# Regrouping the SSD side products of a hybrid SSD / S5 decoder step on one Trainium2 core

## The reference, cut to what matters

```python
cb = einsum('bcqgn,bcsgn->bcqsg', cm, bm)
y_diag = einsum('bcqsgj,bcsgjp->bcqgjp', cb[..., None] * seg, xdt)
states = einsum('bcsgn,bcsgjp->bcgjpn', bm, xdt * decay[..., None])
h = chunk_decay * h + states
y_off = einsum('bcqgn,bcgjpn->bcqgjp', cm, h_prev) * exp(acs)[..., None]
```

## Time and profile before

| | |
|---|---|
| median of 3 runs | 2355.67 us (2355.64 to 2357.68) |
| the profiled execution | 2355.64 us, of which the span from first to last instruction is 2353.9 us |
| PE busy | 2346.1 us, 100% of the span |
| DVE, ACT, POOL busy | 1651.4 us (70%), 1060.0 us (45%), 109.2 us (5%) |
| DMA | 453.95 MB, mean 193 GB/s |
| one iteration of the groups | 100.67 us, from one t = 0 stay to the next (575.66 to 676.33) |

### The profile page before, as it was taken

The page is one execution under the profiler, slowest core; times in us unless marked ns, Lnnn a source line. Parts: engine busy times, 40 slices in busy tenths (PEclk is TensorE's granted clock), DMA queues, the critical chain, the costliest instruction groups (busy, mean ns, idle before and its releaser), DMA issues.

```text
span 2353.9 us, 49580 instructions
## 1 busy us (share of the span) xinstructions
PE 2346.1 (100%) x19158; PEld 2299.7 (98%) x19158; DVE 1651.4 (70%) x3109; ACT 1060.0 (45%) x1583; POOL 109.2 (5%) x202
## 2 busy tenths in 40 slices
PE   9999999999999999999999999999999999999999
PEld 9999999999999999999999999999999999999998
DVE  7798988979888878798956555765555555544444
ACT  6453544535444445646633333554334333333333
POOL 1000000000000002101300000000000000000000
PEclk9999999999999999999999999999999999999999
DMA  7676767677676678566876765555555555555543
GB/s 215 199 225 206 242 189 216 212 214 235 189 225 212 206 239 241 152 194 177 250 204 193 205 211 182 182 171 161 162 169 160 170 162 159 174 197 168 169 159 117
DMA packets 546113, 453.95 MB, mean 193 GB/s; under 512 B 31184, under 2 KB 520112, under 8 KB 545408
## 3 DMA queue, kind: packets, MB, share of 16 engines
q1 hardware_dynamic: 525936, 406.23, 57.4%
q0 software_dynamic: 13392, 34.33, 4.5%
q10 hardware_dynamic: 6624, 11.18, 1.4%
HBM read 412.01 MB, written 38.81 MB: 192 GB/s over the span
## 4 chain that ended last, share of the span: by engine, by line
PE 97%; DVE 2%; issue 0%; ACT 0%; POOL 0%; DVEq 0%; ACTq 0%; POOLq 0%
PE acc L2097 30%; PE acc L2098 29%; PE acc L2099 29%; PE side L2084 1%; PE side L2183 1%; PE side L2235 1%; PE side L2107 0%; DVE cacc L1343 0%; PE side L2400 0%; PE side L2366 0%; PE side L2217 0%; PE acc L2579 0%; PE side L2579 0%; PE side L2577 0%; PE side L2578 0%
## 5 line engine op out<-in xcount | busy, mean ns | idle before, releaser
L1298 DVE TENSOR_TENSOR w_lo<-raw,w_hi 128x1024 fp32r<-128x1024 f32 (+2 forms) x692 | 830.2, 1207 | 513.2 <-ACT w_hi L793 507.7
L793 ACT ACTIVATE w_hi<-raw 128x1024 fp32r<-128x1024 f32 (+2 forms) x692 | 716.6, 1045 | 850.9 <-PE acc L2099 828.4
L2097 PE MATMUL acc<-h_hi,w_hi 128*128 128x288 f32 x3344 | 999.5, 299 | 0.0
L2099 PE MATMUL acc<-h_hi,w_lo 128*128 128x288 f32 x3344 | 986.0, 295 | 0.0
L2098 PE MATMUL acc<-h_lo,w_hi 128*128 128x288 f32 x3344 | 985.2, 295 | 0.0
L2097 PEld LDWEIGHTS acc<-h_hi,w_hi 128*128 128x128 f32 x3344 | 627.8, 188 | 15.5 <-issue 13.3
L2098 PEld LDWEIGHTS acc<-h_lo,w_hi 128*128 128x128 f32 x3344 | 627.4, 188 | 2.2 <-issue 2.2
L2099 PEld LDWEIGHTS acc<-h_hi,w_lo 128*128 128x128 f32 x3344 | 627.8, 188 | 0.0
L2097 PE MATMUL acc<-f_hi,w_hi 128*128 128x288 f32 x698 | 207.0, 296 | 0.0
L2099 PE MATMUL acc<-f_hi,w_lo 128*128 128x288 f32 x698 | 205.7, 295 | 0.0
L2098 PE MATMUL acc<-f_lo,w_hi 128*128 128x288 f32 x698 | 205.4, 294 | 0.0
(11 more groups left out here) (406 smaller groups left out, 2681.1 us busy)
## 6 DMA issues: line engine op xcount, KB each, us to landing
raw<-in_w_in_dram SPq DMA_DIRECT2D x512, 256.0 KB, 3.5
raw<-in_w_ffn_up_dram SPq DMA_DIRECT2D x352, 256.0 KB, 3.4
raw<-in_w_ffn_down_dram SPq DMA_DIRECT2D x160, 256.0 KB, 2.9
raw<-in_w_ssm_out_dram SPq DMA_DIRECT2D x128, 256.0 KB, 3.4
raw<-in_w_glu_dram SPq DMA_DIRECT2D x128, 256.0 KB, 3.7
h<-in_state_ssm_dram SPq DMA_DIRECT2D x32, 512.0 KB, 6.9
out_ssm_sample_dram<-h POOLq DMA_DIRECT2D x32, 512.0 KB, 3.8
raw<-in_w_out_dram SPq DMA_DIRECT2D x64, 256.0 KB, 3.2
```

The source lines that it names most:

```text
L793: copy = lambda out, in_, **k: nc.scalar.activation(out, in_, ACT.Copy, **k)
L1298: tt(w_lo[:, slot, 0:n], raw[:, slot, 0:n], w_hi[:, slot, 0:n].bitcast(F32), ALU.subtract).then_inc(lo_ready, 1)
L2097: mm(o_, wh, xh[:, kt, :], start=first and i == 0, stop=False)
L2099: done = mm(o_, wl, xh[:, kt, :], start=False, stop=last and i == n - 1)
```

## The change

SSD operations move to other steps, and some to other banks. Nothing is added or removed but a few waits.

| | before | after |
|---|---|---|
| PE: turns of the x sample rows | t = 6 | t = 3, alone |
| PE: `within` of blocks 0, 1, 2 | t = 6, 6, 12 | t = 8 (s2, s0, s1) |
| PE: reads of the sample states | t = 12 | t = 8 |
| PE: block 0's state | t = 6, into s1 | t = 10, into s2, alone |
| PE: block 1's reads, block 1's state | t = 8, into s1, s3 | t = 12, into s1, s0 |
| PE: turns of the sample reads | t = 14 | t = 12 |
| ACT: copy of block 0's state; of the sample reads | t = 7; 13 | t = 11; 9 |
| DVE: sample x; mask of block 2; `cm` | t = 7; 7; 10 | t = 5; 6; 7 |
| DVE: skips of blocks 0, 1, 2 | t = 9, 11, 13 | t = 9, 9, 10 |
| DVE: block 1's reads scaled, added; samples' | t = 11, 12; 15 | t = 13, 13; 13 |
| DVE: `ht` decayed and added (`prompt_state_ready`) | t = 10 | t = 14 |
| DVE: decays of the sample states | t = 13 to 16 | t = 11, 12, 14, 15 |
| SP: loads of the sample states | t = 6 to 9 | t = 4 to 7 |

PE's wait for `prompt_state_ready` moves from t = 12 to t = 16. SP's wait for it stays at t = 17.

```diff
@@ -464,8 +464,8 @@
                     conv_history(g + 1)
                 if not ssd:
                     return
-                if 6 <= t < 10:
-                    q = t - 6
+                if 4 <= t < 8:
+                    q = t - 4
                     if g > 0:
                         sp.wait_ge(h0_stored[q], g * 16)
                     sp.dma_start(h0[:, 2 * q:2 * q + 2, :], a['state_ssm'][g, :, 2 * q:2 * q + 2, :]).then_inc(h0_landed[q], 16)
@@ -871,13 +871,13 @@
                     if t == 8:
                         act.wait_ge(sem("xw_ready"), g * 3 + 3)
                         copy(xws[0:32, :], offe[0:32, :]).then_inc(sem("xws_rounded"), 1)
-                    if t == 7:
+                    if t == 11:
                         act.wait_ge(sem("ht_ready"), g + 1)
                         act.wait_ge(sem("bst_ready"), g + 1)
-                        copy(ht[:, :], s1[:, :]).then_inc(sem("ht_copied"), 1)
-                    if t == 13:
+                        copy(ht[:, :], s2[:, :]).then_inc(sem("ht_copied"), 1)
+                    if t == 9:
                         act.wait_ge(sem("h0_read"), g + 1)
-                        act.wait_ge(sem("off1_added"), g + 1)
+                        act.wait_ge(sem("xws_ready"), g + 1)
                         copy(offe[:, :], s3[:, :]).then_inc(sem("read_copied"), 1)
                     if t == 24:
                         act.wait_ge(sem("y_gated"), g + 1)
@@ -1435,7 +1435,7 @@
                     if t == 4:
                         dve.wait_ge(sem("btok_ready"), g + 1)
                         tt(bst[32:64, :], ht[0:32, 0:NS], bst[0:32, :].bitcast(F32), ALU.subtract).then_inc(sem("bst_ready"), 1)
-                    if t == 7:
+                    if t == 5:
                         dve.wait_ge(sem("x2_turned"), g + 1)
                         tt(by_head(xdt[0:32, 2, :]), by_head(s3[0:32, :]), bc(gtv[0:32, DT + 2, :], HD, 2),
                            ALU.mult).then_inc(sem("xdt_ready"), 1)
@@ -1449,43 +1449,43 @@
                         mask(0, g)
                     if t == 5:
                         mask(1, g)
-                    if t == 7:
+                    if t == 6:
                         mask(2, g)
                     if t == 9:
                         dve.wait_ge(sem("y0_ready"), g + 1)
                         wait(dve, "y_summed", g * 3)
                         skip(0, s2, g, par)
-                    if t == 11:
-                        dve.wait_ge(sem("xws_ready"), g + 1)
-                        dve.wait_ge(sem("off1_ready"), g + 1)
-                        dve.wait_ge(sem("decay_landed"), g * 32 + 32)
-                        tt(offe[:, :].rearrange("p (i q) -> p i q", i=4), s1[:, :].rearrange("p (i q) -> p i q", i=4),
-                           ee[:, :, 0:P], ALU.mult).then_inc(sem("off1_scaled"), 1)
                         dve.wait_ge(sem("y1_ready"), g + 1)
                         skip(1, s0, g, par)
-                    if t == 10:
+                    if t == 7:
                         wait(dve, "h0_read", g)
                         cT = xc[:, par, 1, SEQ:T].rearrange("p (r h t) -> p h r t", h=2, t=DL)
                         for h in range(2):
                             last = dve.tensor_copy(cm[:, 4 * h:4 * h + 4, DL * h:DL * h + DL], cT[:, h])
                         last.then_inc(sem("cm_ready"), 1)
+                    if t == 13:
                         dve.wait_ge(sem("off1_ready"), g + 1)
-                        link(tt(by_head(ht[:, :]), by_head(ht[:, :]), bc(gtv[:, CDEC, :], HD, 2), ALU.mult))
-                        dve.wait_ge(sem("prompt_state"), g + 1)
-                        tt(ht[:, :], ht[:, :], s3[:, :], ALU.add).then_inc(sem("prompt_state_ready"), 1)
-                    if t == 12:
+                        dve.wait_ge(sem("off2_ready"), g + 1)
+                        dve.wait_ge(sem("decay_landed"), g * 32 + 32)
+                        tt(offe[:, :].rearrange("p (i q) -> p i q", i=4), s1[:, :].rearrange("p (i q) -> p i q", i=4),
+                           ee[:, :, 0:P], ALU.mult).then_inc(sem("off1_scaled"), 1)
+                        dve.wait_ge(sem("off1_scaled"), g + 1)
                         dve.wait_ge(sem("y_skip"), g * 3 + 2)
                         v = yb[:, :, P:SEQ]
                         tt(v, v, offe[:, :].rearrange("p (i q) -> p i q", i=4), ALU.add).then_inc(sem("off1_added"), 1)
                     if t == 14:
+                        link(tt(by_head(ht[:, :]), by_head(ht[:, :]), bc(gtv[:, CDEC, :], HD, 2), ALU.mult))
+                        dve.wait_ge(sem("prompt_state"), g + 1)
+                        tt(ht[:, :], ht[:, :], s0[:, :], ALU.add).then_inc(sem("prompt_state_ready"), 1)
                         dve.wait_ge(sem("outer_landed"), 16 * (g + 1))
                         tt(bm[:, :, :], bc(xwe[:, 512:].bitcast(F32), 2, 1), bc(hmask[:, 0:2], NS, 2), ALU.mult).then_inc(sem("bm_ready"), 1)
-                    if t == 13:
+                    if t == 10:
                         dve.wait_ge(sem("y2_ready"), g + 1)
-                        skip(2, s2, g, par)
-                    if 13 <= t < 17:
+                        skip(2, s1, g, par)
+                    if t in (11, 12, 14, 15):
                         dve.wait_ge(sem("h0_read"), g + 1)
-                        for u in (2 * (t - 13), 2 * (t - 13) + 1):
+                        first = 2 * (11, 12, 14, 15).index(t)
+                        for u in (first, first + 1):
                             of = bdec[:, SAMPLES[u], g * HG:(g + 1) * HG]
                             tt(by_head(h0[:, u, :]), by_head(h0[:, u, :]), bc(of, HD, 2), ALU.mult).then_inc(sem("h0_decayed"), 1)
                     if t in (17, 18, 21, 22):
@@ -1494,8 +1494,8 @@
                             dve.wait_ge(sem("h0_decayed"), g * DB + u + 1)
                             dve.wait_ge(sem("h0_product"), g * DB + u + 1)
                             tt(h0[:, u, :], h0[:, u, :], product_bank(u)[:, :], ALU.add).then_inc(sem("h0_updated"), 1)
-                    if t == 15:
-                        dve.wait_ge(sem("off2_ready"), g + 1)
+                    if t == 13:
+                        dve.wait_ge(sem("off1_added"), g + 1)
                         tt(offe[:, 0:P].rearrange("p (i r k) -> p i r k", i=4, r=4),
                            s3[:, :].rearrange("p (i r x) -> p i r x", i=4, r=4)[:, :, :, 0:2 * DL],
                            ee[:, :, P:160].rearrange("p i (r k) -> p i r k", r=4), ALU.mult).then_inc(sem("off2_scaled"), 1)
@@ -2204,37 +2204,36 @@
                             for i in range(4):
                                 last = turn((s2, s3)[c][:, i * P:(i + 1) * P], xc[:, par, 2 + i, c * P:(c + 1) * P])
                         last.then_inc(sem("x01_turned"), 1)
-                    if t == 6:
-                        pe.wait_ge(sem("btok_ready"), g + 1)
+                    if t == 3:
                         pe.wait_ge(sem("xdt_ready"), g * 3 + 2)
                         for i in range(4):
                             last = turn(s3[0:32, i * P:(i + 1) * P], xc[:, par, 2 + i, SEQ:T])
                         last.then_inc(sem("x2_turned"), 1)
+                    if t == 8:
+                        pe.wait_ge(sem("btok_ready"), g + 1)
+                        pe.wait_ge(sem("cb_masked"), g + 1)
+                        pe.wait_ge(sem("xdt_ready"), g * 3 + 3)
                         within(s2, 0, g).then_inc(sem("y0_ready"), 1)
                         within(s0, 1, g).then_inc(sem("y1_ready"), 1)
-                        pe.wait_ge(sem("cb_masked"), g + 1)
-                        pe.wait_ge(sem("xw_ready"), g * 3 + 2)
-                        mm(s1[:, :], btok[:, 0, :], xw[:, 0, :], **one).then_inc(sem("ht_ready"), 1)
-                    if t == 8:
-                        pe.wait_ge(sem("ht_copied"), g + 1)
-                        for i in range(4):
-                            last = mm(s1[:, i * P:(i + 1) * P], ht[:, i * P:(i + 1) * P], cT[:, P:SEQ], **one)
-                        last.then_inc(sem("off1_ready"), 1)
-                        pe.wait_ge(sem("xdt_ready"), g * 3 + 3)
-                        mm(s3[:, :], btok[:, 1, :], xw[:, 1, :], **one).then_inc(sem("prompt_state"), 1)
-                    if t == 12:
-                        pe.wait_ge(sem("xdt_ready"), g * 3 + 3)
-                        pe.wait_ge(sem("y_skip"), g * 3 + 1)
-                        within(s2, 2, g).then_inc(sem("y2_ready"), 1)
+                        within(s1, 2, g).then_inc(sem("y2_ready"), 1)
                         pe.wait_ge(sem("cm_ready"), g + 1)
-                        pe.wait_ge(sem("prompt_state_ready"), g + 1)
                         for b in range(DB):
                             if b % 2 == 0:
                                 pe.wait_ge(h0_landed[b // 2], g * 16 + 16)
                             r = b % 4
```

(13 more changed lines are left out.)

## The result

| | before | after |
|---|---|---|
| median | 2357.54 us (2355.64 to 2358.08, 5 runs) | 2395.55 us (2391.70 to 2397.65, 5 runs) |
| ratio, 95% interval | | 1.0166 (1.0155 to 1.0177), slower |
| span of the profiled execution | 2353.9 us | 2390.0 us |
| PE's granted clock, mean, profiled execution | 1.000 | 0.995 |
| one iteration | 100.67 us | 105.5 to 106.0 us |

Slower, as forecast, but by 36.1 us of span where 17.4 were forecast, and outside the range of 2360 to 2390. By the medians it is 38.0 us: the profiled execution is the fastest of the five, and the granted clock of the others was 0.993 or 0.994. The kernel before has two groups of runs, near 2355.7 and near 2357.8 us, and its median of five falls into the upper one.

What follows compares the result with a forecast made beforehand. PE, busy for the whole span, was taken as the bound. Group 0's 2.9, plus 14.6 for iterations 1 to 6, minus 0.1 for group 7, gave +17.4 us on 2355.64: 2373.0, range 2360 to 2390.

Steps and rivals of the forecast that it cites:

- The cause: SP's wait at t = 17 holds chunk 18's load, delaying DVE and PE's restart: +2.4 us in each of iterations 1 to 6.
- PE's stays: PE's time on the moved SSD work per group: 8.14 us before, 8.04 to 8.24 after; gain taken 0.1.
- the turns alone: PE's turns of the x sample rows, alone at t = 3 after the change, priced at 0.53 us.
- the rule on draining: On PE, each change of tiling mode drains the engine; ten changes per group before and after, so no gain.
- the chain: DVE's steps up to `z_silu`: 0.55 us leaves t = 15, 0.3 of the t = 16 decays is gained, together 0.9.
- the landing: Chunk 18's load, issued by SP after the store, lands 3.3 us later (median of 2.5 to 7.1), at 635.3.
- The lag at `z_silu`: DVE's `z_silu` before PE's hand-over starts 3.6 - 0.9 = 2.7 us late, at 675.1.
- The estimate of 2.6 us: Skill's DMA cost model for a 256 KB load: each hand-over 0.7 us sooner, 2368 in all; not adopted.
- my rival of the burst: Released SP queue makes chunks 19 and 20 land late, up to 3.8 us more per hand-over: 2386 to 2400; chance 0.13.
- the clock's rival: After each PE wait the next chunk runs at 1.2 GHz, 3.2 us more seven times, +22: 2395; chance 0.05.
- Group 0: Hand-over where PE already waits: split 4.6 us late, 0.55 and 1.2 come off, +2.9 all on the path.

Runs made afterwards that it cites:

- The late store: Changed kernel with SP's wait for the prompt's state and its store moved from t = 17 to t = 24: 2358.18 us, ratio 1.0009.
- the gate alone: Kernel before, with SP at t = 17 also waiting for the fourth decay of the sample states, nothing else moved: 2396.46 us, ratio 1.0166.
- late acs loads: Changed kernel with SP's four acs loads at t = 22 to 25 instead of 18 to 21: 2383.52 us, ratio 1.0117.
- store at t = 18: Changed kernel with SP's wait and store of the prompt's state at t = 18 instead of t = 17: 2367.24 us, ratio 1.0043.
- only the store behind chunk 18: Changed kernel with SP's wait left at t = 17 and only the store moved behind chunk 18's load, to t = 18: 2397.38 us, ratio 1.0169.
- store in POOL's queue: Changed kernel with the prompt's state wait and store moved from SP's queue to POOL's, ahead of its sample-state stores: 2358.26 us, ratio 1.0009.

## Why the prediction fell short

- **The cause was right**, step by step. The prompt's addition ends 55.4 us from the t = 0 stay, as computed (631.1 - 575.66). SP's wait at t = 17 holds the load of chunk 18, ACT's rounding ends on a DMA, and PE waits for the second z at seven places. The late store and the gate alone show it from both sides.
- **PE's stays** cost 0.44, 4.45, 0.86 and 2.19 us, 7.94 together, against 8.14: a gain of 0.2 per group where 0.1 was taken. The difference is the turns alone, 0.44 where I had priced 0.53. By the rule on draining (TensorEngine Tiling (Array Packing), the Trainium skill, Key Properties) the gain would be nil, as the prediction worked out; the measurement decides.
- **DVE without the gate** starts the split of t = 15 1.5 us later than before (58.7 against 57.2) and `z_silu` 0.65 later, so that 0.9 come off the chain, as computed.
- **The first step that failed is the landing.** I took 3.3 us, the median of loads that come two at a time, for a load that is let go together with a store, four acs loads and three more chunks. The second load of chunk 18 took 4.0 and that of chunk 19 6.4. The split of t = 15 came 4.3 us late in the iteration shown, not 3.6, and chunk 19 was late as well: of the 0.9 us by which the chain is lighter only 0.3 was left. The lag at `z_silu` was 4.04 us (100.74 from the stay, 96.70 before) instead of 2.7, PE's restart 3.77 late instead of 2.4. The estimate of 2.6 us that the prediction sets beside the 3.3 lies further off still. This was my rival of the burst, with a chance of 0.13, at 1.3 us per hand-over where I had given it 1.9 to 3.8. My argument against it, that DVE wants the chunks 3 to 5 us apart, missed that the chunk that comes first is short of time already.
- **The second is the clock**, which the sum put at nothing. It fell after six of seven waits of 3.35 us, at 1.34 us each in the iteration shown. I had this as a rival at 0.05, on the ground that a wait of 0.89 us did nothing, and put it beside the forecast instead of on it. The page TensorE: Matmul & The Clock Gate (the Trainium skill, Why this matters for your kernels) warns of just this, and the trace agrees. The two rivals were not exclusive: the longer wait brings the fall. That the sum of the clock's rival, 2395, is the measured time is luck: it rests on 3.2 us per fall, more than twice what one cost.
- **The sum, by the trace.** PE's restarts after the seven waits come 27.5 us late in all, where 17.5 were forecast (2.9 + 14.6; six times 2.4 is 14.4, so 0.2 of that was a slip). The six falls add 8.2, the first matmul after a restart about 0.1 in six iterations. The last t = 0 stay is then 36.2 late (813.23 against 777.00), the span 36.1. By kind of wait it comes out less well: 23.4 + 1.9 + 1.4 - 0.9 = 25.8, falls 8.2, stays -1.6, together 32.4 of 36.1. The rest fits the 13 waits that are new, near 0.27 us each beyond the idle time shown: a matmul's record lasts 0.29 where the next one starts after 0.13, and the first distance after a wait is 0.24. That reading was not tested by itself.
- **Group 0** was forecast at +2.9 and gave 5.4 (178.39 - 172.96): PE's restart came 4.1 late, and the fall added 1.3.

## What to carry to other kernels

When an operation moves to a later step, look for every wait on its semaphore that does not move with it, above all in a queue that runs ahead: SP runs seven steps ahead here, so that a store that no engine was in a hurry for closed the gate on the weights. Price what is behind such a gate as one burst of all its bytes, not as single transfers. And put a stall of the matrix engine and the fall of its clock into one case, not into two rivals.

## What the runs showed of the hardware

- The clock's answer to a wait of PE is not a function of its length alone. In the changed kernel it fell after six of seven waits of 3.34 to 3.36 us. With the late acs loads it fell after five of seven: after 2.53, 2.70, 2.79, 3.33 and 3.35, not after 2.63 and 2.69. With the gate in the kernel before it fell after six of eight, of 3.10 to 4.28 us, not after 2.57 and 2.94. With the store at t = 18 it fell after one of 2.25 us and not after 2.22 and 2.15.
- A fall can cost twice as much. In the profiled execution with only the store behind chunk 18 all seven waits were 3.32 to 3.34 us; the t = 0 stay began 4.6 to 4.8 us after five of the restarts, and 5.9 us after two (387.16 to 393.08, 707.93 to 713.86). The runs of the changed kernel spread over 6 us; falls of unequal number and cost may be why, which was not tested.
- The clock also fell where PE had no wait: in the profiled executions of the late store and of the store in POOL's queue the only falls before the end are from 2342 us on, with PE busy for 1.99 of 2.00 us. So not every fall comes from a hand-over.
- Behind the gate the DMA engines moved up to 387 GB/s at a share of 1.06, against a mean of 190 over the span.
